# Gate projections of a hybrid decoder layer: 14 of 16 pairs of feature rows as products of half operands, 7 in place of 8

## The reference, cut to what matters

```python
qa, ka, va, qr, kr, vr, gr, gate_a, gate_b = jnp.split(xn @ w_in, splits, axis=-1)
...
r = rms_plain(orr.astype(F32)).reshape(B, T, RET_V_W).astype(dtype) * jax.nn.silu(gr)
ba, bb = jnp.split(b_gate, 2)
m = jax.nn.sigmoid(gate_a + ba) * (a @ w_pa) + jax.nn.sigmoid(gate_b + bb) * (r @ w_pb)
```

## Time and profile before

| what | value |
|---|---|
| median of 3 runs | 2740.68 us (2739.56 to 2742.55) |
| the profiled execution's own time | 2738.75 us |
| its span, first to last instruction | 2737.0 us |
| what lies around the span | 1.75 us |
| mean granted TensorE clock | 0.999 |
| busy: PE, DVE, POOL, ACT | 2706.9, 1368.7, 868.0, 740.8 us |

### The profile page before, as it was taken

How to read it: one execution, slowest core, us unless ns; L and a number is a source line. 1 busy time by engine, 2 the same in 40 slices (tenths; PEclk the granted TensorE clock), 3 DMA queues, 4 the chain that set the end, 5 groups by cost and what they waited for, 6 DMA issues and landing times.

```text
span 2737.0 us, 41596 instructions
## 1 busy us (share of the span) xinstructions
PE 2706.9 (99%) x16114; PEld 2334.2 (85%) x16114; DVE 1368.7 (50%) x2728; ACT 740.8 (27%) x1549; POOL 868.0 (32%) x697
## 2 busy tenths in 40 slices
PE   8999999999999999999999999999999999999998
PEld 6888877777777779888888899999899999998887
DVE  6431355547666655666555533243485555542224
ACT  5111122225555542222222221011332222221012
POOL 2533423302211232221122235354124444455230
PEclk9999999999999999999999999999999999999999
DMA  4323356553333334456554554334122222245221
GB/s 161 113 100 132 107 195 205 196 178 116 99 130 108 106 130 163 160 192 198 188 190 149 191 188 145 126 120 159 47 83 71 76 91 72 72 149 175 87 61 66
DMA packets 277923, 362.14 MB, mean 132 GB/s; under 512 B 28530, under 2 KB 172530, under 8 KB 277746
## 3 DMA queue, kind: packets, MB, share of 16 engines
q1 hardware_dynamic: 277746, 359.74, 39.5%
HBM read 257.24 MB, written 111.35 MB: 135 GB/s over the span
## 4 chain that ended last, share of the span: by engine, by line
PE 95%; DVE 3%; ACT 1%; issue 1%; DMA 0%; POOL 0%; SPq 0%; DVEq 0%; ACTq 0%; POOLq 0%
PE psum L538 24%; PE psum L1334 14%; PE psum L2747 14%; PE psum L2073 12%; PE psum L563 10%; PE psum L1024 3%; PE psum L1046 2%; PE psum L2729 2%; PE psum L2122 2%; PE psum L2106 1%; PE psum L2771 1%; PE psum L1448 1%; PE psum L1036 1%; PE psum L2115 1%; PE psum L1000 1%
## 5 line engine op out<-in xcount | busy, mean ns | idle before, releaser
L364 POOL TENSOR_TENSOR w_h<-stage,ones 128x512 fp32r<-128x512 f32 x268 | 305.6, 1168 | 1297.8 <-PE psum L2073 384.2
L371 POOL TENSOR_TENSOR w_l<-stage,w_h 128x512 fp32r<-128x512 f32 x268 | 359.1, 1367 | 123.3 <-DVE acc L1174 118.6
L538 PE MATMUL psum<-w_h,xt_h 128*128 128x512 f32 x864 | 343.6, 398 | 3.5 <-POOL w_l L385 2.8
L538 PE MATMUL psum<-w_h,xt_l 128*128 128x512 f32 x864 | 341.8, 396 | 0.0
L538 PE MATMUL psum<-w_l,xt_h 128*128 128x512 f32 x864 | 341.8, 396 | 0.0
L2073 PE MATMUL psum<-xt_h,w_h 128*128 128x384 f32 x744 | 263.7, 354 | 0.1
L2073 PE MATMUL psum<-xt_h,w_l 128*128 128x384 f32 x744 | 244.4, 328 | 0.0
L2073 PE MATMUL psum<-xt_l,w_h 128*128 128x384 f32 x744 | 244.3, 328 | 0.0
L416 POOL TENSOR_TENSOR w_l<-stage,w_h 128x512 fp32r<-128x512 f32 x106 | 139.4, 1315 | 268.8 <-ACT w_h L2841 268.8
L1334 PE MATMUL psum<-w_h,xt_h 128*128 128x512 f32 x512 | 219.3, 428 | 0.0
L1334 PE MATMUL psum<-w_l,xt_h 128*128 128x512 f32 x512 | 202.4, 395 | 0.0
(11 more groups left out here) (307 smaller groups left out, 5719.2 us busy)
## 6 DMA issues: line engine op xcount, KB each, us to landing
stage<-in_w_in_dram SPq DMA_DIRECT2D x88, 512.0 KB, 5.6
proj<-edge SPq DMA_DIRECT2D x112, 256.0 KB, 2.1
stage<-in_w_gu_dram SPq DMA_DIRECT2D x88, 256.0 KB, 3.8
out_dram<-acc SPq DMA_DIRECT2D x43, 512.0 KB, 3.7
acc<-proj SPq DMA_DIRECT2D x82, 256.0 KB, 3.1
gates<-edge SPq DMA_DIRECT2D x32, 544.0 KB, 3.4
acc<-in_cache_k_dram SPq DMA_DIRECT2D x32, 512.0 KB, 5.3
acc<-in_cache_v_dram SPq DMA_DIRECT2D x32, 512.0 KB, 4.6
```

Of the source, the lines that this page charges most:

```text
L364: last = nc.gpsimd.tensor_tensor(w_h[s][:, a:b, :], src, one.unsqueeze(1).to_broadcast([128, b - a, WN]), ALU.mult)
L371: last = nc.gpsimd.tensor_tensor(w_l[s][:, a:b, :], stage[h][:, a - lo:b - lo, :], w_h[s][:, a:b, :].bitcast(F), ALU.subtract)
L538: last = nc.tensor.matmul(psum[:, bank, :], x, w[s][:, k, :], start=k == 0 and n == 0, stop=k == nk - 1 and n == len(passes) - 1)
```

## The change: what it does, and the diff

Pairs of rows (256 features) take the place of rows; there are 16, and p is their number from 0. Pairs 0 and 15 are computed as before. For pairs 1 to 14, the weights are a 2 x 2 matrix A of blocks (128 features x 512 of the contraction), and the first 640 tokens a 2 x 2 matrix B (512 of the contraction x 320 tokens). The four result blocks c11, c12, c21, c22 are made of seven products in place of eight, with sums of blocks of A (S1 to S4) and of B (T1 to T4) as operands. The last 448 tokens are computed directly, as one chunk of 448 columns a row. The 48 steps of a pair remain: 7 products of 4 steps, two direct chunks of 8 steps each, and 4 steps without a matmul of the gates (only `sample_piece`).

- PE: a pair is 7 x 4 x 3 = 84 matmuls of 320 columns and 2 x 8 x 3 = 48 of 448, where it was 96 of 384 and 48 of 320.
- T1 to T4 and their high and low parts are made once, during pair 0: for each of four k, 8 operations of 320 columns on DVE, 4 casts on ACT, 4 subtractions on DVE. They lie in the rest of `w_h` and `w_l`. PE waits for all of them at the first product of pair 1 that uses one (its step 28).
- Weights: `load_gate_pair` brings one pair at a time. ACT casts each of the 8 operands of a pair (512 columns); POOL makes the four S in place (4 operations) and 8 low parts. The split tiles of the gates on POOL are gone. Operands lie in 5 slots in turn.
- Results: ACT copies each product out of PSUM to SBUF (7 copies of 320 columns); DVE makes the 8 sums (320 columns, both inputs in SBUF). For p < 8 DVE then multiplies six times (2 of 448, 4 of 320), after sigmoids of ACT; for p >= 8 ACT takes the sigmoid of 640 columns at once. A pair's last block c12 is finished in the next pair's first steps.
- The first merge tile is cast by ACT and split by POOL during pair 15, its last k after the gates' last unit, and the second merge tile is loaded and split after the gates.

The diff, cut to its core:

```diff
+P1, PLAIN0, P2, PLAIN1, P4, P7, P6, P5, P3 = range(9)
+PRODUCTS = {P1: ("A11", "B11"), P2: ("A12", "B21"), P4: ("A22", "T4"), P7: ("S3", "T3"), P6: ("S2", "T2"),
+            P5: ("S1", "T1"), P3: ("S4", "B22")}
...
+        def wait_bank(idx):
...
+                pe.wait_ge(gate_read, idx - 1)
...
+        def fast_pair(p):
+            y = 0
+            for u in range(9):
+                idx = gate_unit(p, u)
+                wait_bank(idx)
+                if u in PRODUCTS:
+                    name, moving = PRODUCTS[u]
+                    o = gate_op(p, name)
+                    pe.wait_ge(op_split, o + 1)
+                    if p == 1 and moving[0] == "T":
+                        pe.wait_ge(t_step, 12)
+                    for k in range(4):
+                        sample_piece(2 * p + y // 24, y % 24)
+                        for n, (wt, low) in enumerate(((gop_h, False), (gop_h, True), (gop_l, False))):
+                            last = nc.tensor.matmul(psum[:, gate_bank(idx), 0:GH], wt(o)[:, k, :], gate_x(moving, k, low),
+                                                    start=k == 0 and n == 0, stop=k == 3 and n == 2)
...
+                        wide_group(p, r, k, idx, GT, T - GT)
...
+        def gate_sum_made(p, name):            # POOL
+            a11, a12, a21, a22 = (gate_source(p, x) for x in GATE_OPS[True])
+            if name == "S3":
+                nc.gpsimd.tensor_tensor(a21, a11, a21, ALU.subtract).then_inc(sums_ready, 1)
...
+        def copy_out(p, u, dst):               # ACT
+            act.wait_ge(gate_full, gate_unit(p, u) + 1)
+            nc.scalar.copy(dst, psum[:, gate_bank(gate_unit(p, u)), 0:GH]).then_inc(gate_read, 1)
...
+            if y == 40:                        # ACT, fast_steps
+                copy_out(p, P6, part_gd)
+            if y == 41:
+                gate_high(act, p + 1, "A21")
+            if y == 43 and p < 8:
+                sigmoid(p, "c21", part_gd, 2 * p + 1, 0)
+            if y == 44:
+                copy_out(p, P5, gate_part(2 * p + 1, GH, GH))
+            if y == 45:
+                gate_high(act, p + 1, "A22")
+            if y == 46 and p < 8:
+                sigmoid(p, "c22", part_gc, 2 * p + 1, GH)
...
+            if y == 41:                        # DVE, fast_steps
+                c21 = gate_part(row1, 0, GH)
+                dve.wait_ge(gate_read, gate_unit(p, P6) + 1)
+                nc.vector.tensor_tensor(b, d, b, ALU.add).then_inc(v_done, 1)
+                dve.wait_ge(v_done, gate_step(p, "v7"))
+                nc.vector.tensor_tensor(c, d, c, ALU.add).then_inc(v_done, 1)
+                dve.wait_ge(v_done, gate_step(p, "u3"))
+                nc.vector.tensor_tensor(c21, c, c21, ALU.subtract).then_inc(v_done, 1)
...
+                    if y == 0 and p >= 2:      # ACT, next pair's step 0
+                        copy_out(p - 1, P3, gate_part(2 * p - 2, GH, GH))
...
-            load_w(sp, W_PB)
+            load_w(sp, W_PA + 1)
```

More of the change, by code:

```diff
@@ L115, in v_step @@
 def v_step(n, name):
-    return len(BY_DVE) + sum(len(v_names(m)) for m in range(n)) + v_names(n).index(name) + 1
+    return len(BY_DVE) + N_GATE_STEPS + sum(len(v_names(m)) for m in range(n)) + v_names(n).index(name) + 1
 def s_step(n, name):
@@ L285, in hybrid_layer @@
     sg_ready = sem("sg_ready")
+    gate_full, gate_read = sem("gate_full"), sem("gate_read")
     gate_ready = sem("gate_ready")
@@ L543, in pe_token_tile, with pe_feature_tile @@
                     behind(t)
-    def pe_feature_tile(pe, xh, xl, s, split, g, order=range(4), free=None, ready=None, beside=None):
+    def pe_feature_tile(pe, xh, xl, s, split, g, order=range(4), free=None, ready=None, beside=None, holder=None):
         for j, m in enumerate(order):
@@ new lines, in wide_group @@
+        def wide_group(p, r, k, idx, a, width):
+            o = gate_op(p, (("A11", "A12"), ("A21", "A22"))[r][k // 4])
+            if k % 4 == 0:
+                pe.wait_ge(op_split, o + 1)
+            for n, (wt, x) in enumerate(((gop_h, xt_h1), (gop_h, xt_l1), (gop_l, xt_h1))):
+                last = nc.tensor.matmul(psum[:, gate_bank(idx), 0:width], wt(o)[:, k % 4, :], x[:, k, a:a + width],
+                                        start=k == 0 and n == 0, stop=k == KD - 1 and n == 2)
+            if k == KD - 1:
+                last.then_inc(gate_full, 1)
@@ new lines, in plain_steps @@
+        def plain_steps(p, y):
+            if p == 0 and y and y % 8 == 0:
+                plain_unit(p, y // 8 - 1)
+            if p and y in (8, 16, 24):
+                plain_unit(p, y // 8 - 1)
+            if p == 0 and y == 1:
+                gate_high(act, 1, "A11")
+            if p == 0 and y in T_HIGH_MARKS:
+                k = T_HIGH_MARKS.index(y)
+                act.wait_ge(t_step, 3 * k + 1)
+                for t in range(1, 5):
+                    last = nc.scalar.copy(tg_piece(t, k, False), tg_sums(t, k))
+                last.then_inc(t_step, 1)
+            if p == 0 and y == 25:
+                gate_high(act, 1, "A12")
+            if p == 0 and y == 26:
+                gate_high(act, 1, "A21")
+            if p and y in PA_MARKS:
+                merge_high(PA_MARKS[y])
```

495 lines of the change are left out of this document (393 added, 102 removed).

## The result

| | kernel before | changed kernel |
|---|---|---|
| median | 2740.62 us (2738.48 to 2742.55, 6 runs) | 2827.22 us (2823.57 to 2830.39, 6 runs) |
| ratio | | 1.0317 (95% interval 1.0306 to 1.0328) |
| profiled span | 2737.0 us | 2824.8 us |
| mean granted clock | 0.999 | 0.982 |
| gate stage, first to last matmul of the gates | 595.5 us | 679.1 us |

What follows compares the result with a forecast made beforehand. PE, busy 99% of the span, was taken as the bound: -26 saved, +3 start, +6 x 1.5 and +7 x 0.8 waits, 0 end, so -8.4 us to 2732.3 us; own range 2724 to 2735, wider range 2718 to 2754.

Steps and rivals of the forecast that it cites:

- PE's work: Gate matmuls at 0.146 us (320 columns) and 0.2035 (448): 1.86 us saved a pair, 26 us over 14 pairs.
- What a sum costs: DVE's new sums in the gate stage: 0.49 us each unhindered, 0.6 us more for six in ten beside POOL.
- DVE's load: DVE busy 32.6 us a pair in pairs 2 to 7 (93% with sigmoid waits), 28.0 in 8 to 14 (78%).
- the 85% I named as the sign: Sign that the forecast is right: DVE busy over 85% in windows of pairs 2 to 7.
- Where PE will wait: At a pair's end, PE waits for its bank: 1.5 us in pairs 2 to 7, 0.8 in 8 to 14.
- the same wait seen elsewhere: Retention reads and casts queued on ACT, masks and low parts on DVE: counted as no second wait, no size added.
- 11.9 us of average work against 11.5 us of time: Pair's end, steps 37 to 52: DVE and ACT work up to P3's copy against 15 PE steps; even on average.
- The start: Making T on DVE and ACT in pair 0, pair 1's first copy: 3 us lost, bounds 0 and 6.
- The end: Merge tiles cast, loaded and split around the gates' end: nothing lost; 2 us if a load is late.
- DVE becomes the bound of pairs 2 to 7: Rival: DVE needs 40.4 us a pair; six pairs lose 10 us, 8 to 14 break even; 2752 us, chance 0.27.
- might spare DVE half of the hits: At the shared SBUF port, DVE coming first makes POOL wait: half the hits free; counted within the 2718 us rival, chance 0.15.

Runs made afterwards that it cites:

- h1: Changed kernel with POOL's sums and low parts on 32 columns, T1 to T4's operations and DVE's eight sums on 8: 0.9989 of the kernel before.
- e5: Changed kernel with POOL's sums and low parts of pairs 1 to 14 on 32 columns, T1 to T4's operations on 8: 1.0029 of the kernel before.
- f2: Changed kernel with v of retention's reciprocal root kept in PSUM, nothing left out: 1.0237 of the kernel before.
- e3: Changed kernel with the 64 operations that make T1 to T4 cut from 320 to 8 columns: 1.0265 of the kernel before.
- e1: Changed kernel with POOL's sums and low parts of pairs 1 to 14 cut from 512 to 32 columns: 1.0065 of the kernel before.
- f1: Changed kernel with DVE's sums reading five products straight from PSUM, ACT's copies of them gone, nothing left out: 1.0245 of the kernel before.
- f3: Changed kernel with DVE's sums reading five products from PSUM and the retention root's v in PSUM: 1.0157 of the kernel before.

## Why the prediction was wrong, by its own steps

- **PE's work: right.** 0.146 and 0.204 us as taken (0.146, 0.2035); 26 us saved.
- **What a sum costs: right.** Taken 0.49 + 0.36 = 0.85 us, measured 0.875.
- **DVE's load: nearly right.** Foreseen 32.6 us a pair in pairs 2 to 7 and 28.0 in 8 to 14; measured 31.3 and 29.4. It was not the bound: DVE never reached the 85% I named as the sign (65 to 73% in pairs 2 to 7, at most 78% in any), since the pairs grew with it.
- **"Where PE will wait": the step that failed.** Taken 1.5 us a pair for pairs 2 to 7 and 0.8 for 8 to 14, bounds 4 and 2. Measured, as length after less length before plus 1.86: pairs 2 to 7 took 267.6 us for 230.5, so 8.0 a pair; pairs 8 to 14 took 297.5 for 272.4, so 5.4. Together 86 us where 14.6 stood. Three things were wrong in it. The chain: I looked at the gates' banks and called retention's waits "the same wait seen elsewhere"; PE waits at retention (L2199, L2326, L2334, L2343), and hardly at a bank. The stretch of the pair was right: of the 62 us that PE is idle in pairs 2 to 14, 48 lie between step 37 of a pair and the fourth step of the next (by the count of gate matmuls before each wait). The way of adding: I set 11.9 us of average work against 11.5 us of time and gave the rest to lumps; but retention passes between PE, ACT and DVE several times a chunk, so lateness of DVE is paid at the next handover, however much DVE idles later. From h1 to the changed kernel, DVE's busy time rises by 148 us and the time by 90: 0.6 us for each, long before DVE is full. That is a mean. Single steps lie between 0.3 (e5 to h1: 11 us for 35) and 1.1 (f2: 22 us for 20, right before the rows PE waits for), so the place counts as well as the amount. And the small operations: the root's ten stand in front of what PE waits for, and I did not count them as ones that POOL can hit.
- **The clock: not foreseen.** The earlier trace rows shows 1.00 throughout, and I took that for given. It cost 36.8 us of the 83.6 by the split above. It is in the 8.0 and 5.4 us a pair already: part of what a wait costs is the slow stretch behind it.
- **The start: mis-sized.** 3 us taken (bounds 0 and 6); pairs 0 and 1 took 78.6 us for 57.8. With the 1.86 us that pair 1 saves, that is 23 us. By e3, making T is 14 of them. In e5, with POOL thin as well, the two pairs take 58.9 us, so POOL is 6 more, and 3 are left.
- **The end: 0 taken.** The two profiled executions differ by 87.8 us, of which 4.2 lie outside the stage; the merge waited 2.7 us for POOL's w_l (L672 <- L509).
- **The rivals.** "DVE becomes the bound of pairs 2 to 7" had the right sign and the wrong mechanism: pairs 2 to 7 lose 37 us net, not 10, with DVE at 65 to 73%, and pairs 8 to 14, which it left even, lose 25. Its 2752 us was 11 us of the 87. That the Trainium skill's rule (SBUF — State Buffer, Who interferes with whom) might spare DVE half of the hits did not come about: in the timeline DVE and POOL take turns, and both are stretched.

The causes by runs, in us of the changed kernel's 87 plus the 26 saved, so 113: POOL's contention 69 (e1), making T 10 more (e5), the eight sums' own time 11 more (h1), and 23 with none of them. The shares hang on this order: taken out first, T is 14 (e3) and the sums are 30 (e7). Without anything left out, f1 and f2 win back 44 of the 69; that the rest of e1's gain is at operations that they leave with both inputs in SBUF, or is paid back in f1's waits for banks, is argued and not shown.

What the 23 us of h1 are is not settled. By the same book-keeping as above they are 13 us of PE's idle time and 10 of its clock, but no run tells the order of DVE's queue (whether it would help to put the sums behind what PE waits for) from ACT's new copies and casts. Nor is it settled why the clock falls after some waits and not after others of the same length.

## What to carry to other kernels

A cost that is small in an engine's busy share is not small if that engine stands in a loop of handovers with the bound engine: take lateness at the next handover, not the average, and look which instructions stand in front of the one that is waited for, down to those of one column. Before work goes to POOL beside a busy DVE, list DVE's operations with both inputs in SBUF; putting one input in PSUM took the whole hit off those operations without any work left out (f1, f2). It did not save this change: f3 is still 43 us slower than the kernel before, and a bank that DVE has to free is a new wait for PE. And a saving on a PE that is 99% busy has more to lose than the waits themselves: 14 of them were followed by some us at half clock.
